# Spreading a row-norm factor over the partitions by two small transfers instead of products with the identity

## The reference

```
def rmsnorm(x, g):
    xf = x.astype(jnp.float32)
    y = xf * lax.rsqrt(jnp.mean(xf * xf, axis=-1, keepdims=True) + EPS)
    return (y * g.astype(jnp.float32)).astype(x.dtype)

h = rmsnorm(x, norm_mix[layer])
qa, ka, va, fa, qb, kb, vb = _split(h @ w_in, SPLIT_AB)        # layer 2
log_f = jax.nn.log_sigmoid((fa + b_forget).astype(jnp.float32))
qc, kc, vc, c_q, c_kv, k_r = _split(h @ w_in, SPLIT_CD)        # layer 3
```

## Time and profile before

| | us |
|---|---|
| median of 3 runs | 1039.29 (1038.85 to 1039.87) |
| the profiled execution's own time | 1039.85 |
| its span | 1038.1 |
| TensorE busy | 1028.1 |
| VectorE busy | 719.7 |
| ScalarE busy | 581.1 |
| granted TensorE clock | 0.999 |

### The profile page before, as it was taken

How to read it: one execution, slowest core, us unless ns; L and a number is a source line. 1 busy time by engine, 2 the same in 40 slices (tenths; PEclk the granted TensorE clock), 3 DMA queues, 4 the chain that set the end, 5 groups by cost and what they waited for, 6 DMA issues and landing times.

```text
span 1038.1 us, 16297 instructions
## 1 busy us (share of the span) xinstructions
PE 1028.1 (99%) x5808; PEld 877.4 (85%) x5808; DVE 719.7 (69%) x1156; ACT 581.1 (56%) x871; POOL 1.0 (0%) x8
## 2 busy tenths in 40 slices
PE   9999999999999999999999999999999999999997
PEld 7998788788888888888878888888998878888886
DVE  6898669687766556578776756665678669555664
ACT  6655575674645444464666545444569757444542
POOL 0000000000000000000000000000000000000000
PEclk9999999999999999999999999999999999999999
DMA  8855445455565557547424755656364336665541
GB/s 278 290 170 182 142 142 183 161 181 185 179 207 184 200 189 234 172 137 263 141 70 138 250 193 182 200 183 195 121 192 162 123 122 208 203 208 191 183 141 40
DMA packets 53846, 184.96 MB, mean 178 GB/s; under 512 B 6000, under 2 KB 9504, under 8 KB 53792
## 3 DMA queue, kind: packets, MB, share of 16 engines
q1 hardware_dynamic: 52736, 183.17, 53.8%
q10 hardware_dynamic: 1056, 1.06, 0.3%
HBM read 183.14 MB, written 1.07 MB: 177 GB/s over the span
## 4 chain that ended last, share of the span: by engine, by line
PE 97%; DVE 1%; DMA 1%; ACT 1%; issue 0%; SPq 0%; ACTq 0%; DVEq 0%
PE ps L443 19%; PE ps L444 18%; PE ps L445 18%; PE ps L877 15%; PE ps L880 8%; PE ps L485 3%; PE ps L561 3%; PE ps L649 2%; PE ps L488 2%; PE ps L852 2%; PE ps L673 1%; PE ps L855 1%; DMA raw<-stream 1%; DVE wlo L1655 0%; DMA x<-x_in 0%; PE ps L542 0%
## 5 line engine op out<-in xcount | busy, mean ns | idle before, releaser
L1655 DVE TENSOR_TENSOR wlo<-raw,whi 128x1024 fp32r<-128x1024 f32 x338 | 409.8, 1222 | 159.9 <-ACT whi L1183 156.7
L1183 ACT ACTIVATE whi<-raw 128x1024 fp32r<-128x1024 f32 x338 | 353.2, 1057 | 177.8 <-PE ps L445 120.6
L443 PE MATMUL ps<-whi,y_hi 128*128 128x512 f32 (+1 forms) x524 | 206.2, 394 | 0.0
L444 PE MATMUL ps<-wlo,y_hi 128*128 128x512 f32 (+1 forms) x524 | 203.6, 388 | 0.0
L445 PE MATMUL ps<-whi,y_lo 128*128 128x512 f32 (+1 forms) x524 | 203.5, 388 | 0.0
L877 PE MATMUL ps<-hT,whi 128*128 128x512 f32 x696 | 173.8, 392 | 0.0
L877 PEld LDWEIGHTS ps<-hT,whi 128*128 128x128 f32 x696 | 126.3, 189 | 23.4
L445 PEld LDWEIGHTS ps<-whi,y_lo 128*128 128x128 f32 x524 | 98.4, 188 | 20.6
L443 PEld LDWEIGHTS ps<-whi,y_hi 128*128 128x128 f32 x524 | 98.5, 188 | 19.2 <-issue 0.5
L444 PEld LDWEIGHTS ps<-wlo,y_hi 128*128 128x128 f32 x524 | 98.6, 188 | 18.5
L880 PEld LDWEIGHTS ps<-hT,wlo 128*128 128x128 f32 x696 | 94.9, 190 | 6.8
(11 more groups left out here) (274 smaller groups left out, 1142.7 us busy)
## 6 DMA issues: line engine op xcount, KB each, us to landing
raw<-stream SPq DMA_DIRECT2D x338, 512.0 KB, 3.8
x<-x_in SPq DMA_DIRECT2D x2, 512.0 KB, 4.1
arena<-scratch ACTq DMA_DIRECT2D x1, 1024.0 KB, 12.7
arena<-rb SPq DMA_DIRECT2D x1, 1024.0 KB, 6.4
bm<-decay SPq DMA_DIRECT2D x1, 1024.0 KB, 6.3
out<-arena SPq DMA_DIRECT2D x2, 320.0 KB, 2.2
cst<-const SPq DMA_DIRECT2D x1, 520.0 KB, 7.0
raw<-stream SPq DMA_DIRECT2D x2, 256.0 KB, 4.5
```

The lines of the kernel that those rows point to most:

```text
L443: pe.matmul(o, a[0], b[0], start=start, stop=False)
L444: pe.matmul(o, a[0], b[1], start=False, stop=False)
L1183: act.activation(whi[:, u % RING, :], raw[:, u % RAW, :], ACT.Copy).then_inc(sem("hi_done"), 1)
L1655: dve.tensor_tensor(wlo[:, u % RING, :], raw[:, u % RAW, :], whi[:, u % RING, :].bitcast(F32), ALU.subtract).then_inc(sem("lo_done"), 1)
```

## The change

`spread_rs` and `keep_rsB` go. ScalarE stores the two columns of `rs` to a scratch tensor in DRAM, 128 pieces of 4 bytes each, waits until both have landed, and loads the 256 numbers to all 128 partitions (128 KB, rows of 1 KB). In layer 2 the stores stand in u = 0, behind `hi` and ahead of the evacuation of `fa`; the load stands in u = 2, ahead of `hi(base + 8)`. In layer 3 the stores stand ahead of the first `hi` of the loop, the load at the start of u = 2. VectorE waits for the load at u = 3 in both layers. In layer 2 `wide_sum("fq", 0)`, the gate, its Exp and Ln, and the scan move one unit later (u = 2 to 3, and 3 to 4).

```diff
--- before.py
+++ after.py
@@ TensorE
-            def spread_rs(i):
-
-                pe.wait_ge(sem("n_rs"), i)
-                pe.wait_ge(sem("n_lo"), 8 * i + 4)
-                for t in range(TT):
-                    m = pe.matmul(ps[:, W3, t * P:(t + 1) * P], rs[:, t:t + 1].to_broadcast([P, P]), cs(C_ID),
-                                  start=True, stop=True)
-                m.then_inc(sem("rsB_ps"), 1)
-
@@ layer 2, loop over u
-                if u == 2:
-                    spread_rs(1)
@@ layer 3, between()
-                    if u == 3:
-                        spread_rs(2)
@@ ScalarE
+            def send_rs(i):
+
+                act.wait_ge(sem("n_rs"), i)
+                for t in range(TT):
+                    act.dma_start(bass.AP(scratch.tensor, 400 * i + t * P, [[1, P], [1, 1]]),
+                                  rs[:, t:t + 1]).then_inc(sem("rs_out"), 16)
+
+            def fetch_rs(i):
+                act.wait_ge(sem("rs_out"), 16 * TT * i)
+                act.dma_start(rsB, bass.AP(scratch.tensor, 400 * i, [[0, P], [1, S]])).then_inc(sem("rs_in"), 16)
+
@@ layer 2, loop over u
                 steps(steps_ab_v, u, 0)
+                if u == 2:
+                    fetch_rs(1)
                 hi(base + u + LEAD)
+                if u == 0:
+                    send_rs(1)
                 steps(steps_ab_v, u, 1)
...
-                if u == 2:
+                if u == 3:
                     act.wait_ge(sem("fx_e"), 1)
                     link(act.activation(fe, fe, ACT.Exp))
                     act.activation(fe, fe, ACT.Ln, bias=bias1[0:8]).then_inc(sem("fx_ln"), 1)
@@ layer 3, loop over u
             for u in range(n3):
+                if u == 0:
+                    send_rs(2)
                 if u == 2:
+                    fetch_rs(2)
                     act.wait_ge(sem("c_in"), 16)
@@ VectorE
-            def keep_rsB(i):
-                dve.wait_ge(sem("rsB_ps"), i)
-                link(dve.tensor_copy(rsB, ps[:, W3, 0:S]))
-
@@ layer 2, loop over u
-                if u == 2:
-                    keep_rsB(1)
-                if u in (2, 4, 6, 8):
-                    wide_sum(*{2: ("fq", fq, 0, 0.125), 4: ("fq", fq, 1, 0.125), 6: ("fk", fk, 0, 1.0),
+                if u == 3:
+                    dve.wait_ge(sem("rs_in"), 16)
+                if u in (3, 4, 6, 8):
+                    wide_sum(*{3: ("fq", fq, 0, 0.125), 4: ("fq", fq, 1, 0.125), 6: ("fk", fk, 0, 1.0),
                                8: ("fk", fk, 1, 1.0)}[u])
...
-                if u == 2:
+                if u == 3:
 
                     dve.wait_ge(sem("evac"), evac_no["fa"] + 1)
                     link(dve.tensor_tensor(fz, fa[0:8, :], rsB[0:8, :], ALU.mult))
...
-                if u == 3:
+                if u == 4:
                     dve.wait_ge(sem("fx_ln"), 1)
@@ layer 3, loop over u
-                if u == 2:
-                    keep_rsB(2)
                 if u == 3:
+
+                    dve.wait_ge(sem("rs_in"), 32)
                     evac_v("sq", sq, 0.125)
```

## The result

The changed kernel takes 1055.61 us (median of 4 runs, 1055.24 to 1056.84); beside it the kernel before takes 1039.58 us. The ratio is 1.0158 (1.0146 to 1.0170). Forecast were 1038.9 us and no difference that can be measured, with a range that ended at 1041.4. The forecast of the median was 16.7 us too low, and the difference from the kernel before came out with the other sign.

A forecast was written before the change was run, and what follows sets the result against it. TensorE, holding 97% of the chain, was taken as the bound. Layer 2 at 0.55 - 0.44 = 0.1 us slower and layer 3 at 0.44 us gained gave -0.35 us: median 1038.9 from 1039.29, range 1038.0 to 1041.4.

The forecast's parts named there:

- step 7: Layer 2, fk's first unit: TensorE waits about 0.55 us for the add of fq, done at 459.0 with 0.05 for release.
- step 2: Layer 2, ScalarE: two store issues from 451.3 to about 452.4 delay the evacuation of fa; dead heat, 0.05 us counted.
- rival 3: ScalarE's issue of 128 pieces takes over 1 us, stalling TensorE 1 us or more at layer 2's third unit; about 1040.3; chance 0.05.
- step 8: Layer 2, after the first add: three later TensorE demands on VectorE hold, by 0.1, 1.2 and 0.25 us; nothing more counted.
- The removed pairs: TensorE, layers 2 and 3: the spread_rs products taken out, 0.44 us gained in each layer, 0.88 us in all.
- Step 3: Layer 2, landing of the small stores: taken as 2.2 us, with 3.96 us from above and 0.57 us as floor.
- F: Layer 2: the moment the stores of the factor have landed, forecast at 454.1 on the profiled run's clock.
- rival 2: Layer 2, VectorE's wait on rs_in ahead of fk: costs more than the products did, a stall over 0.88 us; chance 0.23.
- Step 5: Layer 2, the fetch of the factor to 128 partitions: lands after 3.8 us, at 457.95; bounds 2.2 and 6.3 us.
- The sum: Whole kernel: layer 2 0.1 us slower, layer 3 0.44 us gained, together -0.35 us; median after 1038.9 us.
- no loss: Layer 3: evac_v("sq") begins later but TensorE's bank is ready with over 3 us left; gain 0.44 us.
- extreme case: Layer 2, store landing and fetch both at their upper bounds: stall of 4.5 us, median 1042.9 us.

The follow-up runs named there:

- the probes: Kernel before with extra transfers of varied spacing, size and target on ScalarE's queue in the first block, nobody waiting until the end; 1043.1, 1039.5 and 1040.6 us.

## Why the prediction was wrong

*Which bound, and which place: right.* TensorE's program sets the time; the loss in layer 2 is VectorE's wait on `rs_in` with `fk`'s first unit behind it (step 7). Its sum, fed with the measured start of the add, gives 465.64 + 0.75 - 458.05 = 8.3 us (458.05 is its 458.48 in a trace that runs 0.42 us ahead); the trace has 8.24, or 8.3 by the later products. The two issues took 0.93 us, 1.1 in step 2, TensorE did not wait for the evacuation of `fa` behind them, and rival 3 fell. The three later deadlines of step 8 held: layer 2 shows no second gap. In the changed kernel the slow clock gave them 1.7 us more than their 0.1 to 1.2; but with the waits filled, at full clock, they held too (the second add ended at 471.46, the unit that needs it began at 471.67). The removed pairs were worth 0.44 us each, as forecast.

*Step 3, the landing of the stores: the step that failed.* "No row shows the landing of a store of 128 pieces of 4 bytes" was true. But the upper bound beside it, 3.96 us, was taken from a store of 8 pieces of 1 KB, and the lower one from a large store; neither has many small pieces side by side. The landing took 8.13 us behind the second issue, not 2.2. F came at 459.40, not 454.1, in a trace that runs 0.42 us ahead: 5.7 us late, of a stall that was forecast at 0.55 and measured at 8.24. A row that resembles an operation in bytes alone does not bound it. I also let the rule of the Trainium skill, "SBUF — State Buffer", section "The DMA setup-cost knee", of about 2 us for any transfer, stand near my number; it holds here for stores whose pieces start 32 bytes apart or more (1.4 to 2.4 us where nothing stood ahead) and misses this one by 6. The other, the Trainium skill, "DMA: Bandwidth & Descriptors", section "Specifications", on writes under 512 bytes, pointed the right way, and I gave it 0.23 with rival 2. But its 512 bytes are not the point that counts here: 4-byte pieces 32 bytes apart are quick.

*Step 5, the fetch: 6.2 and 4.8 us against 3.8.* Within its bounds, 2.4 us of the miss in layer 2. With the stores left out it took 3.7 (median), with quick ones 3.2, so part of the excess may be the loads that landed late beside the slow stores. It may also be that the fetch reads what has just been written, in pieces: both quick fetches read another row. That was not separated.

*The sum: a term is missing.* I priced no clock. Each gap on TensorE brought slow products behind it: 1.66 us in layer 2 and 2.62 in layer 3. A stall of 8.24 us was in truth one of 9.9.

*Layer 3: "no loss" was wrong.* I followed the one bank that `evac_v("sq")` frees, and it did hold. I did not follow the row of VectorE and ScalarE work that stands behind the same wait up to TensorE's next demand on it, `y_lo` at u = 10. With a landing of 7.9 us it cost 4.01. Nor was it safe within my own bounds: with the row in SBUF the stores took 2.1 us and the spreading 6.4, less together than the 3.96 and 6.3 with which I had seen "over 3 us left", and TensorE waited 2.2 us for `y_lo`.

*Rival 2* named the right mechanism, the right place and the right cause, and its extreme case, 1042.9, was 12.7 us too low for the three reasons above: the landing, the clock, and layer 3.

## What to carry to other kernels

Before a column goes to DRAM as neighbouring elements of 4 bytes, look for a row with pieces of that form. If there is none, the upper bound is open, and the chance for slower has to say so. Put the wait for a transfer where the waiting engine has nothing behind it that others need soon, and follow the whole row of work behind the wait, on each engine, to TensorE's next demand. Add the clock to the gaps that TensorE gets: here 1.6 to 2.6 us behind each wait of 2.2 to 8.2 us that was looked at, and nothing behind the one of 1.70 us (granted clock 1.00).

## What the runs showed of the hardware that I had not expected

Stores of 128 pieces of 4 bytes to DRAM landed in 7.2 to 8.6 us side by side, two at once in up to 10, and in 1.4 to 2.4 us with starts 32 bytes apart or more, when nothing stood ahead of them. 64 pieces took as long as 128, 16 took 2.3. The same column into one partition of SBUF took 2.0 us in the kernel and 3.4 to 4.2 in the probes. All landings in the probes are single ones.

While such a store is under way, other queues' loads land late. In the changed kernel's window of 450 to 467 the four weight loads (512 KB each) have a median of 6.9 us; in the same window it is 3.7 before, 4.1 with the stores left out and 4.4 with their pieces 512 bytes apart. The two issued while the stores were under way, at 452.54 and 454.63, took 10.0 and 9.2, and the two behind them 4.4 in the median:

```profile
raw<-stream SPq DMA_DIRECT2D x4, 512.0 KB, 6.9
...
raw<-stream SPq DMA_DIRECT2D x1, 512.0 KB, 10.0
...
raw<-stream SPq DMA_DIRECT2D x1, 512.0 KB, 9.2
```

The probes show the same: the load behind a lone slow store took 9.4, 9.1 and 8.8 us in the three runs. Slow stores are not alone in this: in the kernel with the row in SBUF the three loads issued beside the spreading took 7.3 to 8.0 us.

The late landings fit the Trainium skill, "DMA: Bandwidth & Descriptors", section "Queues, rings and completion order", by which a landing is signalled only behind every earlier write of the same DMA engine, of all its queues; the rows show the delay and not its cause.

Spreading a row of 1 KB over 128 partitions took 6.4 to 6.8 us out of one partition of SBUF. Out of DRAM it took 2.9 to 4.2 where the row had stood there all along, in the probes once 5.3, and 4.8 and 6.2 in the changed kernel, right behind the slow stores.

Open: why neighbouring starts under 32 bytes are slow (it is measured, not explained), why 64 such pieces take as long as 128, and why the fetch behind the slow stores is slow.
